# Stick-breaking attention, one pair of heads at a time: projection pieces spread over three accumulator banks, output halves added at the end, low parts of queries and keys on GpSimd

## The reference

```
z = q @ k.T * scale ; mask = key < query
log_keep = where(mask, log_sigmoid(-z), 0)
later = reversed cumulative sum of log_keep, without the own term
a = where(mask, exp(log_sigmoid(z) + later), 0)
out = a @ v
```

## Time and profile before

| | |
|---|---|
| median of 3 runs | 2794.26 us (2794.18 to 2794.43) |
| the profiled execution, its own time | 2795.82 us |
| its span, first to last instruction | 2794.2 us |
| TensorE clock granted, mean | 0.982 |
| busy: PE, DVE, ACT, POOL | 95%, 51%, 38%, 18% of the span |
| first seven pairs | from about 1411 to 1900.8 us |
| last pair | 1900.8 to 1958.7 us |

### The profile page before, as it was taken

How to read it: one execution, slowest core, us unless ns; L and a number is a source line. 1 busy time by engine, 2 the same in 40 slices (tenths; PEclk the granted TensorE clock), 3 DMA queues, 4 the chain that set the end, 5 groups by cost and what they waited for, 6 DMA issues and landing times. The chain is left out here.

```text
span 2794.2 us, 35231 instructions
## 1 busy us (share of the span) xinstructions
PE 2665.1 (95%) x12704; PEld 2217.7 (79%) x12704; DVE 1429.5 (51%) x1773; ACT 1050.4 (38%) x1719; POOL 504.7 (18%) x425
## 2 busy tenths in 40 slices
PE   7999999999999999998989999997998999999999
PEld 7888888877888878887877777776787888887887
DVE  6453444276444451314667777777337644444131
ACT  6451003134333330215656666665323433333020
POOL 2200000102223220003023333332011322321000
PEclk9999999999999999998999999998999999999999
DMA  6411111122232252104111111111312223226111
GB/s 204 143 31 45 45 46 52 52 91 93 96 105 81 99 192 89 52 22 150 54 29 31 31 30 30 30 30 63 136 45 98 95 100 105 86 79 238 46 52 71
DMA packets 57414, 221.44 MB, mean 79 GB/s; under 512 B 7280, under 2 KB 7280, under 8 KB 52080
## 3 DMA queue, kind: packets, MB, share of 16 engines
q1 hardware_dynamic: 43920, 164.68, 17.6%
q0 software_dynamic: 13120, 49.29, 5.1%
q10 hardware_dynamic: 288, 6.29, 0.6%
HBM read 170.43 MB, written 49.81 MB: 79 GB/s over the span
## 5 line engine op out<-in xcount | busy, mean ns | idle before, releaser
L1765 PE MATMUL ps<-xg_hi,w_hi 128*128 128x512 f32 x1344 | 544.0, 405 | 52.0 <-DVE up L1219 17.3
L1767 PE MATMUL ps<-xg_hi,w_lo 128*128 128x512 f32 x1344 | 529.5, 394 | 0.0
L1766 PE MATMUL ps<-xg_lo,w_hi 128*128 128x512 f32 x1344 | 529.3, 394 | 0.0
L1765 PE MATMUL ps<-tile_hi,g_hi 128*128 128x512 f32 x1064 | 419.8, 395 | 12.9 <-DVE up L1691 12.4
L1767 PE MATMUL ps<-tile_hi,g_lo 128*128 128x512 f32 x1064 | 417.5, 392 | 0.0
L1766 PE MATMUL ps<-tile_lo,g_hi 128*128 128x512 f32 x1064 | 415.4, 390 | 0.0
L1765 PEld LDWEIGHTS ps<-xg_hi,w_hi 128*128 128x128 f32 x1344 | 255.9, 190 | 109.4 <-issue 28.0
L1767 PEld LDWEIGHTS ps<-xg_hi,w_lo 128*128 128x128 f32 x1344 | 255.4, 190 | 56.0
L1766 PEld LDWEIGHTS ps<-xg_lo,w_hi 128*128 128x128 f32 x1344 | 256.4, 191 | 47.6 <-issue 0.7
L1765 PE MATMUL ps<-act_hi,d_hi 128*128 128x512 f32 x704 | 276.7, 393 | 0.0
L1767 PE MATMUL ps<-act_hi,d_lo 128*128 128x512 f32 x704 | 275.7, 392 | 0.0
(11 more groups left out here) (211 smaller groups left out, 4108.5 us busy)
## 6 DMA issues: line engine op xcount, KB each, us to landing
raw<-wpack SPq DMA_DIRECT2D x108, 512.0 KB, 3.6
quads<-wpack SPq DMA_DIRECT2D x38, 1024.0 KB, 5.5
d_raw<-wpack SPq DMA_DIRECT2D x32, 704.0 KB, 4.2
stage<-d_act POOLq DMA_DIRECT2D x44, 512.0 KB, 6.6
d_act<-up SPq DMA_DIRECT2D x38, 256.0 KB, 2.1
d_act<-gate SPq DMA_DIRECT2D x38, 256.0 KB, 2.3
d_x<-x SPq DMA_DIRECT2D x16, 512.0 KB, 6.5
x<-d_x SPq DMA_DIRECT2D x16, 512.0 KB, 4.8
```

Source lines behind the costliest of these rows:

```text
L1765: pe.matmul(out, whi, mhi, start=start, stop=False, skip_group_check=chained)
L1766: pe.matmul(out, whi, mlo, start=False, stop=False, skip_group_check=chained)
L1767: return pe.matmul(out, wlo, mhi, start=False, stop=stop, skip_group_check=chained)
```

## The change

- The pieces 0 to 5 accumulate in banks 3, 7, 1, 3, 7, 1. A piece in bank 3 or 1 waits for the sigmoids that read that bank's scores last; z of a row with over 512 keys waits for the evacuation of the piece that was in its bank.
- `FILL` is new: item 0 and item 4 have eight steps in place of six, items 1, 2 and 5 one less, item 6 two less, item 7 one more.
- For the first seven pairs ACT copies all 128 rows of bank 6 (`o_full`), POOL stores both halves to DRAM, and no engine adds them in the pair. In the last pair POOL loads the two halves as `mx` and `mx_low` (four transfers in item 0, four in item 1) and adds them by seven operations of 128 x 1024 in items 4 to 7.
- `lo_part` of the next pair moves from DVE to POOL: behind the store in items 1 and 2, ahead of it in items 4 and 5.

```diff
-        FILL = [(3, 3), (2, 2, 2), (4, 1, 1, 1), (0, 2, 1, 1, 1), (3, 3), (2, 2, 2), (4, 2, 1, 1), (0, 4, 0, 0, 0)]
+        FILL = [(4, 4), (2, 2, 1), (3, 1, 1, 1), (0, 2, 1, 1, 1), (4, 4), (2, 2, 1), (3, 1, 1, 1), (1, 4, 0, 0, 0)]
+        PIECE_BANK = (3, 7, 1, 3, 7, 1)
...
+                    def lo_part(hp, to, piece, weighed):
+                        part, half = piece // 2, ln[piece % 2]
+                        pool.wait_ge(a_ready, weighed)
+                        for hh in range(2):
...
+                            pool.wait_ge(sqk_hi_ready, hp * 12 + ((2, 4)[part] * piece - 4 * part + hh + 1))
+                            pool.tensor_tensor(lo, tf[rows, half], fp(hi), ALU.subtract).then_inc(sqk_lo_ready, 1)
+                            pool.wait_ge(sqk_lo_ready, hp * 8 + (2 * piece + hh + 1))
...
+                            if not last and it in (4, 5):
+                                lo_part(hp + 1, 1 - par, it - 2, hp * ROWS + (2 * it + 4))
                             if not last:
...
+                                pool.wait_ge(o_full_ready, hp * ITEMS + (it + 1))
+                                pool.dma_start(d_mix[bass.ds(hp, 1), it // 4, :, toks].rearrange("a p c -> (a p) c"),
+                                               o_full[:, it % 2, :]).then_inc(so_stored[it % 2], 16)
+                                if it in (1, 2):
+                                    lo_part(hp + 1, 1 - par, it - 1, hp * ROWS + (2 * it + 4))
+                            elif it < 2:
...
+                                for t in (mx, mx_low):
+                                    for hh in range(2):
...
+                            elif it >= 4:
+                                for m in range(2 * it - 8, min(2 * it - 6, KB - 1)):
+                                    pool.wait_ge(mx_loaded[m // (KB - 2)], 64)
+                                    pool.tensor_tensor(mx[:, m, :], mx[:, m, :], mx_low[:, m, :], ALU.add
+                                                       ).then_inc(mx_summed, 1)
...
+                                if not (first and it < 2):
+                                    act.wait_ge(so_stored[it % 2], hp * (8 * ITEMS) + 16 * (it // 2))
+                                act.activation(o_full[:, it % 2, :], ps[:, 6, 0:2 * P], ACT.Copy
+                                               ).then_inc(o_full_ready, 1)
...
                                 if not last and (it, n) in ENDS:
-                                    project(hp + 1, ENDS[it, n])
+                                    project(hp + 1, ENDS[it, n], PIECE_BANK[ENDS[it, n]])
...
+                                free = hp * ROWS + (ROWS // 2 * (piece // 3) - ROWS)
...
+                                    pe.wait_ge(sig_ready, free + (ROWS // 2 - 1))
...
+                                if not last and (it, r) in ((1, 1), (5, 0), (5, 1)):
+                                    pe.wait_ge(evacuated, hp * 6 + (v0 + 6 + (1 if it == 1 else 3 + r)))
```

More of the change, by code:

```diff
@@ L356, in trunk @@
         vT_lo_ready = sem("vT_lo_ready")
-        mx_loaded = sem("mx_loaded")
+        mx_loaded = [sem(f"mx_loaded{p}") for p in range(2)]
+        mx_summed = sem("mx_summed")
         me_loaded = sem("me_loaded")
@@ L655, in weigh, with pair @@
                                            keep[:, par, r, 1:n], ALU.mult).then_inc(a_ready, 1)
-                    def pair(hp, last):
+                    def pair(hp, par, last):
                         for it in range(ITEMS):
@@ L978, in pair @@
                             act.wait_ge(pv_done, hp * CHUNKS + CHUNKS_BEFORE[it + 1])
[L979 to L982, removed]
+                            if last:
+                                if it > 0:
+                                    act.wait_ge(o_sum_ready, it)
+                                act.activation(o_low[rows, :], ps[SHEAD:P, 6, 0:2 * P], ACT.Copy
+                                               ).then_inc(o_low_ready, 1)
+                            else:
+                                if not (first and it < 2):
+                                    act.wait_ge(so_stored[it % 2], hp * (8 * ITEMS) + 16 * (it // 2))
+                                act.activation(o_full[:, it % 2, :], ps[:, 6, 0:2 * P], ACT.Copy
+                                               ).then_inc(o_full_ready, 1)
                             if not last and it in (1, 2):
@@ L1508, in pair @@
                                 dst = mx[rows, KB - 1, t * 2 * P:(t + 1) * 2 * P]
[L1509 to L1518, removed]
+                                dve.wait_ge(o_low_ready, it + 1)
+                                dve.tensor_tensor(dst, ps[0:SHEAD, 6, 0:2 * P], o_low[rows, :], ALU.add
+                                                  ).then_inc(o_sum_ready, 1)
                     for piece in range(6):
@@ L1996, in z, with project @@
                         pe.matmul(o[:, w - P:w], ident_r[:], mask_r[:], start=False, stop=True).then_inc(z_full, 1)
-                    def project(hp, piece, ks=range(KB), first=False):
+                    def project(hp, piece, ks=range(KB), first=False, start=False):
                         part, h = piece // 2, piece % 2
@@ L2005, in project @@
                             if not first:
-                                pe.wait_ge(evacuated, hp * 6 + (v0 + piece))
-                                if piece == 0:
+                                free = hp * ROWS + (ROWS // 2 * (piece // 3) - ROWS)
+                                if piece % 3 == 0:
+                                    if piece == 0:
+                                        pe.wait_ge(evacuated, hp * 6 + v0)
+                                    if piece == 3 or not start:
+                                        pe.wait_ge(sig_ready, free)
+                                elif piece == 1:
                                     pe.wait_ge(vT_lo_ready, hp * 2)
+                                elif piece == 4:
+                                    pe.wait_ge(evacuated, hp * 6 + (v0 + 2))
+                                else:
+                                    pe.wait_ge(sig_ready, free + (ROWS // 2 - 1))
                         for k in ks:
                             c = slice(k * P, (k + 1) * P)
-                            last = three(ps[:, piece if first else 7, :], w_hi[s][:, c], w_lo[s][:, c],
+                            last = three(ps[:, piece if first else PIECE_BANK[piece], :], w_hi[s][:, c], w_lo[s][:, c],
                                          xg_hi[:, k, ln[h]], xg_lo[:, k, ln[h]], k == 0, k == KB - 1)
@@ L2063, in fill @@
                                 k1 = min(k + n, KB)
-                                project(hp + 1, piece, range(k, k1))
+                                project(hp + 1, piece, range(k, k1), start=first)
                                 steps[0] += k1 - k
```

53 lines of the change are left out of this document (30 added, 23 removed).

## The result

The changed kernel takes 2824.55 us (median of 4 runs, 2822.66 to 2826.48), the kernel before 2794.35 us beside it on the same chip. The ratio is 1.0109, 95% interval [1.0097, 1.0122]: slower by 30 us, where I had forecast 2778.0 and a range up to 2791. The span of the profiled execution grew by 30.6 us, from 2794.2 to 2824.8. By starts of PE's matmuls, the seven pairs took 19.8 of them (510.8 where they took 491.0), the last pair 8.9 (66.3 for 57.4), the stretches before and behind 2.

The account below looks back on a forecast made before the run. PE, busy 95% of the span, was taken as the bound, losing time in pairs to latency. Seven pairs gave -20.3 us, the last pair +4.0: -16.3 from the median 2794.3 made 2778.0 us, range 2760 to 2791.

Parts of the forecast that it names:

- The low parts on POOL: Eight subtractions a pair moved to POOL, 1.3 us each, 10.4 in all; claimed hidden up to 2.2 us each.
- GpSimd becomes the bound: slower: Rival, chance 0.08: low parts at 3.5 us on POOL delay weighs in items 4 and 5; 2814 us.
- The walk by stretches: Each of seven pairs cut at PE's anchors into six stretches, changes summed: -2.9 us a pair, -20.3 in all.
- Stretches 1, 2 and 6: From z at 1621.39 to 1637.55, -0.74 us; on to 1647.83, -0.58; from 1682.77 to the next z, +0.59.
- Stretch 3: From item 3's transpose at 1647.83 to z at 1656.27: DVE relieved, shorter waits for aT_lo, -0.65 us.
- stretch 5: From 1672.46 to the transpose at 1682.77: two steps less, tf wait gone, new waits for the chain, -0.83 us.
- stretch 4: From z at 1656.27 to 1672.46: one step more, two waits gone, new 0.7 us wait for the 768 row, -0.69.
- all comes back: Rival, chance 0.10: PE waits for weighed rows and aT_lo as long as for tf; about 2793 us.
- the waits do not come back: Rival, chance 0.13: none of the 5.8 us a pair returns as waits for the softmax chain; 2757.6 us.
- The last pair: Seven additions on POOL in items 4 to 7 slow DVE's weighing of second rows: +4.0 us (0 to +8).
- meetings: In the last pair, three DVE-weighed rows each collide with a POOL addition, nearer 1.3 us each; up to 7.5 in all.
- the additions block the last pair: Rival, no separate chance: loads not there by item 4, or weighs queue behind them; +8 for +4, 2782 us.

Follow-up runs that it names:

- low_on_dve: The changed kernel with the low parts of queries and keys back on DVE; new banks, FILL and late halves stay: 2787.34 us, ratio 0.9973 to the kernel before.
- banks_alone: The kernel before with only the pieces in banks 3, 7 and 1 and the new FILL: 2779.20 us, ratio 0.9944.
- halves_alone: The kernel before with only the output halves stored and added in the last pair: 2802.37 us, ratio 1.0024.

## Why the prediction was wrong

**The low parts on POOL: the step that failed.** I took eight at 1.3 us, hidden up to 2.2. Alone they take 1.28, so the price was right; the mean is 1.67, still below 2.2; and they cost 5 us a pair (72.97 against 67.90 in low_on_dve). The test "hidden while the mean is below the room" was the error: it priced POOL's time, and not what a POOL read does to DVE. I had used the exclusion, shown by the earlier trace rows, for `w_lo` and the last pair's L1492 only. The scan takes two SBUF inputs as well: its call names the row `keep` as both, which the profile prints once. The kernel before had POOL weigh between the scans mostly; a low part put after a weigh falls on the next scan, in both directions. My rival "GpSimd becomes the bound: slower" had the sign, and a time (2814) 10 us short, with another mechanism: it was to decide only from 2.9 us each on.

**The clock was no term of the sum.** The rows said 1.00 in a pair, and I let it stay. PE is busy 461.3 us over the seven pairs and 446.9 with the low parts on DVE, so of the 35.5 us between these two versions 14 are a longer busy time for the same matmuls, and 21 are PE standing idle. The rows show the lower clock behind the waits (eight transposes in 1.83 us for 1.09) as a cause of the 14; that it is the only one is not shown.

**The walk by stretches** is best held against banks_alone and low_on_dve, where the low parts do no harm. Measured from PE's timelines, change of each stretch in us (mean of five pairs, anchors as in the prediction, at the last matmul of z):

| stretch | 1 | 2 | 3 | 4 | 5 | 6 | sum |
|---|---|---|---|---|---|---|---|
| predicted | -0.74 | -0.58 | -0.65 | -0.69 | -0.83 | +0.59 | -2.9 |
| banks_alone | -0.66 | -0.62 | -0.45 | -0.07 | -0.64 | +0.70 | -1.7 |
| low_on_dve | -0.65 | -0.62 | -0.45 | -0.29 | -0.62 | +0.69 | -1.9 |
| the change | -0.65 | +0.79 | +0.08 | +0.06 | +0.82 | +1.94 | +3.0 |

Stretches 1, 2 and 6 came out within 0.11 us. Stretch 3 and stretch 5 were taken 0.2 too good, stretch 4 by 0.4 to 0.6: the wait for the row of 768 keys is 0.97 us there, not 0.7; the rest of that difference I did not resolve. In seven pairs, the first with its own start included, the walk said -20.3; banks_alone gained 14.4, low_on_dve 15.8, by their profiles. The rival "all comes back" is out, and so is "the waits do not come back": of the 5.8 us of waits for `tf` and bank 7, 4.1 came back as others or stayed in a regular pair of banks_alone, where the walk had 2.9. The table's last line shows where the low parts act: stretches 2 and 5, which hold the longest row's chain, and stretch 6. "z waiting for a piece's evacuation" did not come true with the new `FILL`, and did, up to 2.1 us, with the old one.

**The last pair** was +4.0 (0 to +8) and came to +8.9. Three parts of that step were mis-sized. The transfer: I scaled 12.3 us for half the bytes to 25 and had it end 29 us into the pair; single transfers took up to 31.0 us to land, and the additions could start 36.4 us into it. The additions: from 2.35 us to 4.32 beside DVE, against my 2.49. And the "meetings" were counted for three rows of L1492 (one took 3.18 us for 1.22) but not for the scans (3.60 us for 2.02), nor for POOL's weighs, which were to have "over 1 us of room". The nearest of my rivals was "the additions block the last pair", at +8, by the mechanism it named: loads not there by item 4, weighs queued behind.

**The halves in the pairs**, costed at nothing, gave 0.2 to 0.8 us a pair. Over seven pairs that is less than the last pair lost.

**Left open.** Some 2 us of the 30.6 lie behind the attention in the change and in halves_alone (837.9 and 837.5 us from the last addition of outputs to the end, against 835.6 before), but not in low_on_dve; no run looked into it.

The best of these versions that computes the whole reference is banks_alone, at 2779.20 us 0.56% faster than before and 1.6% faster than the change.

## What to carry to other kernels

Before work moves from DVE to POOL, list DVE's instructions with two SBUF inputs, scans among them, and see in a timeline which of them would run beside it: what it can cost is the rest of the partner's run, whatever its own length. An engine with idle time in the windows can still have none at the moments that count, and a short instruction ahead of one on the critical chain can hold it up for the length of its blocker. Change one part at a time where three are bundled: here one gave 15 us and another took 37 back.

## What the hardware showed that I had not expected

- A POOL subtraction of eight columns, 0.20 us alone, took 1.89 us beside a scan, and cost a pair 3.2 us when there were 32 of them; eight memsets at the same places cost nothing.
- Transfers from DRAM to 64 partitions each moved about half as much in a microsecond as one to 128. The windows of the change and of the kernel before, both with the DMA engines full (DMA share 1.02 or 1.03, GB/s last):

```profile
1930.00:1957.00 27.00, 17.82 (x108) 15.71 (x108) 22.44 (x27) 16.03 (x31) 3.74 (x5) 0.87 1.03 213
```

```profile
1915.00:1920.00 5.00, 1.75 (x13) 1.34 (x11) 4.96 (x5) 2.32 (x3) 1.76 (x1) 0.99 1.02 419
```

  The Trainium skill ("SBUF — State Buffer", Door 1: The DMA port swizzle) has partitions 0 to 63 reach 8 of the 16 ports, with about half the rate; 213 against 419 GB/s agrees. The prediction did not weigh it, though the diff loads each half of 64 rows by itself.
- Behind waits of 1.90 and 0.61 us in front of PE, the granted clock was 0.72 over 6 us (1727 to 1733), in a kernel whose pairs had run at 1.00 before the change.
